# Two more feed-forward pairs by seven half-size products, a reordered hand-over, and norm sums inside a loop

## The reference, cut to what matters

```
h = rmsnorm(x, norm_ffn_pre)
u = dwconv3(h @ w_up, conv_w)            # w_up: 1024 x 5632; width-3 convolution over the tokens
gate, val = split(u, 2)                  # 2816 = 22 x 128 columns each
x = x + rmsnorm((silu(gate) * val) @ w_down, norm_ffn_post)
h2 = rms_norm(x, l0_norm); proj = h2 @ w_in_2      # the second block's first projection
```

## Time and profile before

| what | us |
|---|---|
| median of 3 runs | 1787.15 |
| lowest, highest | 1786.33, 1787.56 |
| the profiled execution's own time | 1786.32 |
| its span, first to last instruction | 1784.4 |
| PE busy in the span | 1751.6 |

### The profile page before, as it was taken

How to read it: one execution, slowest core, us unless ns; L and a number is a source line. 1 busy time by engine, 2 the same in 40 slices (tenths; PEclk the granted TensorE clock), 3 DMA queues, 4 the chain that set the end, 5 groups by cost and what they waited for, 6 DMA issues and landing times.

```text
span 1784.4 us, 21029 instructions
## 1 busy us (share of the span) xinstructions
PE 1751.6 (98%) x8288; PEld 1436.9 (81%) x8288; DVE 1195.2 (67%) x1275; ACT 771.2 (43%) x984; POOL 523.4 (29%) x217
## 2 busy tenths in 40 slices
PE   8999999999999999999999999999999999999997
PEld 5778888887888888888788888787788888888786
DVE  7454677848697978878764674764576767676533
ACT  5332222255333555555432433422256666666522
POOL 3457554454121000000264345054421111211051
PEclk9999999999999999999999999999999999999999
DMA  5223222154311122222364355312301111102232
GB/s 185 112 96 118 78 77 83 37 163 151 123 71 72 59 83 94 72 83 94 130 218 148 118 190 176 130 54 77 107 30 36 36 48 36 47 12 71 89 130 94
DMA packets 59434, 170.79 MB, mean 96 GB/s; under 512 B 7632, under 2 KB 8016, under 8 KB 59344
## 3 DMA queue, kind: packets, MB, share of 16 engines
q1 hardware_dynamic: 41488, 120.67, 20.5%
q10 hardware_dynamic: 17856, 48.87, 7.4%
HBM read 131.24 MB, written 38.27 MB: 95 GB/s over the span
## 4 chain that ended last, share of the span: by engine, by line
PE 88%; DVE 6%; ACT 4%; issue 1%; DMA 1%; POOL 0%; ACTq 0%; DVEq 0%
PE psum L671 22%; PE psum L975 15%; PE psum L988 13%; PE psum L710 7%; PE psum L1099 5%; PE psum L1120 5%; PE psum L1156 5%; PE psum L1051 4%; PE psum L870 3%; PE psum L1109 3%; PE psum L692 1%; PE psum L1076 1%; DVE ptl L2341 1%; ACT pth L1714 1%; PE psum L816 1%
## 5 line engine op out<-in xcount | busy, mean ns | idle before, releaser
L583 POOL TENSOR_TENSOR wl<-wstage,wh 128x1024 fp32r<-128x1024 f32 x101 | 262.1, 2597 | 245.8 <-ACT wh L1246 205.5
L578 POOL TENSOR_TENSOR wh<-wstage,ones 128x1024 fp32r<-128x1024 f32 x52 | 126.0, 2423 | 549.0 <-PE psum L1099 307.4
L671 PE MATMUL psum<-hh,wh 128*128 128x512 f32 x608 | 194.1, 400 | 0.9 <-ACT root L1249 0.9
L671 PE MATMUL psum<-hl,wh 128*128 128x512 f32 x608 | 187.6, 390 | 0.0
L671 PE MATMUL psum<-hh,wl 128*128 128x512 f32 x608 | 187.3, 389 | 0.0
L583 POOL TENSOR_TENSOR wx<-wstage,wx 128x1024 fp32r<-128x1024 f32 x25 | 61.6, 2465 | 378.2 <-ACT wx L1246 378.2
L2099 DVE SCALAR_TENSOR_TENSOR cc<-uu,col,cc 128x1023 f32<-128x1023 f32 x88 | 128.8, 1463 | 49.0 <-ACT cc L1462 47.4
L671 PEld LDWEIGHTS psum<-hh,wh 128*128 128x128 f32 x608 | 112.2, 188 | 29.4 <-issue 6.0
L671 PEld LDWEIGHTS psum<-hl,wh 128*128 128x128 f32 x608 | 114.1, 188 | 24.2
L671 PEld LDWEIGHTS psum<-hh,wl 128*128 128x128 f32 x608 | 114.1, 188 | 24.2
L2341 DVE TENSOR_TENSOR ptl<-psum,pth 128x1024 fp32r<-128x1024 f32 x64 | 78.3, 1224 | 55.4 <-ACT pth L1714 55.4
(11 more groups left out here) (362 smaller groups left out, 4365.0 us busy)
## 6 DMA issues: line engine op xcount, KB each, us to landing
wstage<-w_units SPq DMA_DIRECT2D x161, 512.0 KB, 3.8
acts<-cc ACTq DMA_DIRECT2D x22, 512.0 KB, 2.6
hhf<-acts SPq DMA_DIRECT2D x27, 256.0 KB, 4.2
mix<-spill ACTq DMA_DIRECT2D x12, 512.0 KB, 2.6
resid<-yo SPq DMA_DIRECT2D x24, 256.0 KB, 2.0
hlf<-acts SPq DMA_DIRECT2D x17, 256.0 KB, 4.0
kq<-mix SPq DMA_DIRECT2D x16, 256.0 KB, 4.1
gates<-gspill ACTq DMA_DIRECT2D x8, 512.0 KB, 2.6
```

The lines of the kernel that those rows point to most:

```text
L578: pool.tensor_tensor(high, stage(u), ones[:, :].unsqueeze(1).to_broadcast([P, 8, P]), ALU.mult).then_inc(w_high, 1)
L583: pool.tensor_tensor(low, stage(u), high.bitcast(F32), ALU.subtract).then_inc(w_split, 1)
L671: mm = pe.matmul(out[:, t], w[:, wslot, b, :], x[part][:, xk, t], start=start and n == 0, stop=stop and n == 2)
```

## The change

`SP` goes from 7 to 5, so 17 of 22 pairs are made by seven products. The order of the switch is changed on ScalarE and VectorE: T4, and with it the evacuation and centre tap of the last old gate unit, come behind the operands of P6, P5 and P7. The jobs of `LATER` are put into four steps. T1 and T3 are rounded one pair earlier. In `next_layer` the ones-matmuls stand between k steps, and those of the second half come for both n behind k = 5. At the end of the last pair C12 is taken before the taps.

```diff
-SP = 7
+SP = 5
-SW_MADE = ("T1", "T3", "B11", "B21", "T4", "T2", "B22")
+SW_MADE = ("T1", "T3", "B11", "B21", "T2", "T4", "B22")
         def ring(u):
-            return (u + 1) % RING
+            return (u - U_L0 + 1) % RING
...
             if U_DOWN <= u < U_DOWN + DEEP:
-                return product_done(FT - 1, ("P5", "P5", "P2", "P5", "P4")[u - U_DOWN])
+                return product_done(FT - 1, ("P5", "P5", "P5", "P4", "P2")[u - U_DOWN])
...
             def next_layer(n, base, places, emptied, after, sum_bank, y_sum):
                 pe.wait_ge(*emptied(sum_bank))
-                norm_sum_half(n, 0, sum_bank)
+                if n == 2:
+                    norm_sum_half(n, 0, sum_bank)
                 for j in range(4):
...
                     for k in range(KT):
+                        if n == 1 and j == 0:
+                            pe.wait_ge(h_lo, KT + k + 1)
                         mm = half_products(bank(2 * j), places[j], k, 0, k == 0, k == KT - 1)
+                        if n == 1 and (j, k) == (0, 1):
+                            norm_sum_half(n, 0, sum_bank)
                         if (j, k) == after:
                             pe.wait_ge(*emptied(7))
                             sum_half(1, 7, *y_sum)
...
-                pe.wait_ge(half_tile, n)
-                norm_sum_half(n, 1, 0)
+                    if k == 5:
+                        pe.wait_ge(half_tile, n)
+                        norm_sum_half(n, 1, 0)
                 pe.wait_ge(half_root, 2 * n)
...
-                       lambda bk: (evac, E_OUT + KT + TILE_BANK.index(bk) + 1), (0, 1), 3,
+                       lambda bk: (evac, E_OUT + KT + TILE_BANK.index(bk) + 1), (0, 3), 3,
```

ScalarE's stream:

```diff
+                if p == 2:
+                    right_high("T1", KT + 1, (unit_done, U_FF + 5))
                 if p == 3:
-                    right_high("T1", KT + 1, (unit_done, U_FF + 5))
-                if p == 4:
                     right_high("T3", KT + 2)
...
             right_high("B11", KT, (halves_done, 1))
             right_high("B21", KT)
-            right_high("T4", KT + 4, (sw_lo, made("B11", 1)))
-            old_centre(SP - 1, 0)
             product_high(SP, "P6")
             product_high(SP, "P5")
             right_high("T2", KT + 3, (unit_done, U_SW))
             product_high(SP, "P7")
+            right_high("T4", KT + 4, (sw_lo, made("B11", 1)))
+            old_centre(SP - 1, 0)
             product_high(SP, "P4")
             snap(SP, 0)
             old_centre(SP - 1, 1)
```

VectorE's stream:

```diff
-            LATER = (((0, 1), (2, 3)), ((4, 5), (6, 7)), ("T1", "T3"), ("T2", "T1 low"), ("T4", "T3 low"))
+            LATER = (((0, 1, 2, 3), (4, 5, 6, 7)), ("T1", "T3"), ("T2", "T1 low"), ("T4", "T3 low"))
...
             right_low("B11", 0, 1)
             right_low("B21", 0, 1)
-            right_low("T4", 0, 1)
-            projected(SP - 1, 0)
             product_low(SP, "P6")
             product_low(SP, "P5")
             right_low("T2", 0, 1)
             product_low(SP, "P7")
+            right_low("T4", 0, 1)
+            projected(SP - 1, 0)
             product_low(SP, "P4")
             projected(SP - 1, 1)
...
             taken_part(FT - 1, "C22")
             a_low(0)
+            taken_part(FT - 1, "C12")
             taps(FT - 1, 1, 0)
             a_low(1)
-            taken_part(FT - 1, "C12")
             taps(FT - 1, 0, 1)
```

## The result

The changed kernel takes **1791.26 us**, the median of 11 runs (1790.4 to 1792.6); the kernel before took 1786.85 us on the same chip (11 runs, 1786.05 to 1787.57). The ratio is 1.0025 with an interval of 1.0017 to 1.0033: slower by 4.4 us, with 24 matmuls fewer. The prediction was 1791.8. The profiled execution took 1791.1, its span is 1789.3.

The account below looks back on a forecast made before the run. PE, busy 98% of the span, was taken as the bound, at 0.227 us a matmul. -5.4 - 1.1 + 9.7 + 1.6 = +4.8 on 1786.32 gave 1791.1, with 0.8 for the median 1791.8 us; range 1784.5 to 1795.5.

Parts of the forecast that it names:

- The matmuls, -5.4: Two more pairs by seven products: 12 matmuls fewer each, 24 x 0.227 us, so -5.4 us.
- The norm sums, -1.1: In `next_layer` at n = 1, PE's stall on the last square and its restart go: -1.1 us; n = 2 worth 0.
- VectorE, E = 540.5: Before the switch, VectorE's jobs spread over four old pairs, the fourth `gated_unit` ending at 540.5.
- The switch, +9.7: First product to 61st matmul: 23.9 us instead of 14.15, of it 7.8 idle before P6, 0.8 before P1, the rest clock.
- T: The time PE reaches its first product at the switch, predicted 544.6.
- the floor of ScalarE's chain: At the switch, ScalarE's work alone lets the copy for P6 end no sooner than T + 9.8.
- The clock's price: Behind the wait before P6, a slow stretch loses 1.6 us; without it the sum would be 0.9 less.
- The tail, +1.6: End of the last pair: C12's wait goes, but taps beside GpSimd's splits delay step k = 1 to 884.7, +1.6 us.
- VectorE is early: Rival at the switch: E before 536.5, ScalarE's floor holds, 1784.5 to 1786.8 us; chance 0.18.
- the tail's bad case: End of the last pair: a split falls between the taps, +1.6 us; otherwise -0.7.
- The copy not late: Rival at the switch: the stall before P6 is under 1 us, 1779.4 us; chance 0.10.
- Worse: Rival: slow stretches after the switch and after the wait at step k = 1, or E two us later: 1793.5 to 1796; chance 0.12.

Follow-up runs that it names:

- run 10: Run 9's kernel with SP = 7 again, so 15 pairs by seven products and 24 matmuls more: 1787.08 us, ratio 1.0003.
- run 9: Run 8's kernel with the gains of the first 512 tokens applied while VectorE is idle before the last norm's root: 1780.69 us, ratio 0.9972.
- run 2: The changed kernel with the first bank copy, for P6, ahead of T4 and the centre tap on ScalarE: 1792.11 us, ratio 1.0029.
- run 3: The changed kernel with P4's high part and the first copy ahead of T4, the second behind T4, both before the centre taps: 1791.68 us, ratio 1.0026.
- run 7: The changed kernel with the eight gains on only 64 of 1024 tokens, the others left out: 1787.45 us, ratio 1.0001.
- run 11: The changed kernel with the early gains of run 9 and no other edit, nothing left out: 1787.16 us, ratio 1.0002.
- run 5: The changed kernel with the old order at the switch on ScalarE and VectorE, but SP = 5: 1790.31 us, ratio 1.0022.
- run 6: The changed kernel with 30 matmuls into an unused bank in front of P6, keeping PE at work: 1791.88 us, ratio 1.0023.
- run 4: The changed kernel with C12 behind `a_low(1)` at the end of the last pair, as before: 1789.22 us, ratio 1.0013.
- run 8: The changed kernel with copies and next pair's operands ahead of the old unit's work, and C12, `a_low(1)`, taps at the end: 1785.87 us, ratio 0.9989.
- run 1: The kernel before with only the norm-sum edits in `next_layer`: 1785.3 us, ratio 0.9994.

## Why the prediction was right

**The matmuls, -5.4.** 24 fewer in the page; the products from 572 to 868 run some 1306 matmuls in 296.00 us, 0.227 each, with VectorE busy 237 of them (a window's count takes in those that lap over its edges, here 1308; so do the 337 and 1166 of the earlier trace rows, which the prediction divides to 0.226). Run 10 against run 9 is the clean test: -6.4 measured in the median.

**The norm sums, -1.1.** The wait is gone, and the sum on the last square's row comes at 436.99 without idle. The second half's sum stands at 469.18; less the 1.1 us of the later start it is 468.1, the predicted 468.1. The reciprocal at 471.82 is 470.7 in the prediction's count, as predicted. For n = 2 the edit is worth nothing, as put down: the stretch in which it lies is 0.1 longer.

**VectorE, E = 540.5.** `gated_unit` ends at 541.2; with the later start 540.1 in the prediction's count. In between, again less the 1.1 us, the first gain starts at 475.85 (475.85 predicted), and the jobs of pairs 0 to 2 end at 497.1, 510.0 and 527.1 (497.4, 510.4, 527.4). The gains beside splits and without are 10.22 + 4.87 = 15.1 us, against 9.6 + 5.7 put down, and the two splits of pair 2 fall on its taps as written.

**The switch, +9.7: measured +9.5.** T was 545.74 (544.6 and the 1.1 of the start), the copy ended at 559.2 (T + 13.5, predicted T + 14.1), P6 started at 559.32, after 7.34 us of wait (7.8). The first product came 0.56 us after T, with 0.40 of idle for B11 (0.8). The clock behind the wait was at 0.50 for nine matmuls 0.43 apart, 1.8 us (1.6 put down). The 61st matmul had no wait of its own, since PE came later than VectorE's low part; the prediction had them 0.7 us apart the other way and then let P7's end set it, which is what happened. T + 23.7 against T + 23.9. Runs 2 and 3 show that the copy is the first of three things late, runs 7 and 11 that the lateness is VectorE's down to the floor of ScalarE's chain.

One thing in the prediction's account of the switch does not hold. It has the change's new order add the long chain (T4 behind T2, T2 behind the last old unit). Run 5 has the old order and waits 6.7 us. The size came out right because the prediction also took VectorE as late, and with VectorE this late such a wait stands in either order, 7.3 us in the new one and 6.7 in the old. The new order's own part is the floor, the 4.4 us that are left in runs 7 and 11 with VectorE early. That the old order would leave less is likely, since the copy of the kernel before is done 4.2 us behind T (592.84 and 0.58 long, T = 589.26), but it is not shown: no run has the old order, `SP = 5` and an early VectorE together.

**The clock's price.** Behind the wait 1.8 us are lost by the rows, but run 6, which has no slow stretch there, gets only 1.0 us earlier to P1, as VectorE comes next. The prediction had that too: 0.9 less without a slow stretch. By the Trainium skill ("TensorE: Matmul & The Clock Gate", Part 1: The HAM clock gate) the slow stretch behind a long idle is certain, since it has the throttled state as the default; the profiles of the runs with 4.4, 6.0, 6.5, 6.7 and 7.3 us of idle all have it. After the 2.25 us at 888.41 there is none, 24 matmuls in 5.72 us, but behind the same wait runs 3 and 6 have one.

**The tail, +1.6: measured +1.2.** C12 frees the bank in time and both taps meet a split, as put down; 6.29 us against 6.5. Step k = 1 starts at 883.28 before, where the prediction's working had 883.1. Run 4 undoes the edit and gets 2.0 us back in the median, 1.2 of it by its waits. The Trainium skill ("SBUF — State Buffer", Who interferes with whom) has GpSimd share a port pair with VectorE under a lock; two taps of 6.29 us beside splits of 2.41 and 2.91, against 2.60 without a split, agree with the sharing, and so do taps of 4.62 and 4.61 beside splits of 3.44 and 3.50. Who held the ports when, no row shows.

**What was luck.** The terms as measured are -5.4, -1.1, +9.5 and +1.2, with the -0.2 between them +4.0, against the +4.8 that was put down. The rest of the profiles' 4.8 belongs to the executions and not to the change: the later start (+1.1), the absent slow stretch at 1291 (-1.6), the slower end of the span (+1.0), and some 0.3 in small pieces. That profiles and prediction agree to a tenth is luck; the difference of the medians, 4.4, lies between the 4.0 and the 4.8. Also, +4.8 on 1786.32 and the 0.8 make 1791.9 and not 1791.8.

**The rivals.** "VectorE is early" was made true in runs 7 and 11: 1787.45 and 1787.16, where the prediction's bounds for it were 1784.5 to 1786.8. They are 0.7 and 0.4 us outside the upper one, which is for the tail's bad case, the one these runs have. "The copy not late" was priced at 1779.4; run 9 comes near it with 1780.69. It took more than moving the copy: the prediction priced that rival as if one place were late, and three were. "Worse" was two slow stretches, one after the switch and one after the wait at step k = 1: the profile of run 3 has just these two.

## What to carry to other kernels

A reordering that serves one consumer must be read to the end of the queue. Ask for each instruction that it passes, and for those behind, when the next reader needs it. Here PE stood 7.3 us for a 0.6 us copy behind a tap, and moving the copy alone uncovered two more waits of 6.5 and 6.0. When a wait moves without shrinking, the late engine is further up. Look for idle time on it before the last dependency, and fill that with the part of its work that does not depend on it: eight operations more there and the orders of run 8 turned a ratio of 1.0025 into 0.9972. Cutting PE's work also cuts the cover of the engines that run beside it, so count the jobs that must fit before the hand-over along with the matmuls saved.

## What the runs showed of the hardware

The stretches at the lower clock differ from execution to execution with the same instructions. At the start of the span the granted clock rises, and the distance of the matmuls halves, near 11.5 us before and near 13.7 us after; at the same matmul the difference is 1.1 us (31.94 and 33.05). Over all thirteen profiles the rise lies between 11.5 and 14.5 us.

Every wait of PE of 4.4 to 7.3 us, in seven profiles, was followed by a slow stretch, with six to ten distances of 0.43 us between matmuls. Short ones were followed by one in some executions only. Behind the wait of 2.2 to 2.3 us at step k = 1 of `down`, the profiles of runs 3 and 6 have eight slow matmuls, those of the changed kernel and of runs 2, 5, 7 and 11 none. Behind the wait of 1.8 us near 1290, the profiles of the kernel before and of runs 6, 7 and 10 have eight, run 5 has them behind the next wait of 1.8 us, and the other eight none. The changed kernel, at the start and behind its wait of 1.8 us (for which the window 1290 to 1296 above has PEclk 1.00):

```profile
33.05 0.64 PE L702 MATMUL psum<-xin,rkw 128*32 128x512 f32 x4
...
1295.26 0.47 PE L1105 MATMUL psum<-knh,qnh 128*128 128x512 f32 x1 [1.82 <-DVE knl L2347]
```

Each such stretch costs 1.2 to 2.0 us, so two of them are about the spread of a kernel's runs (1.8 us in run 10's eleven, 3.2 in run 8's). That they make the spread is a reading: only one execution of each kernel has a profile. The Trainium skill ("TensorE: Matmul & The Clock Gate", Part 1) says that the number of slow matmuls at a kernel's start varies from run to run with the gate's phase; the thirteen starts here agree.

It also limits what could be shown. Run 6 removed about 1 us at the switch, and in its profiled execution two later slow stretches took 3.2 us. Whether removing one stretch makes a later one more likely stays open: run 10, whose switch has no long wait either, has one at 1291, and runs 1, 8 and 9 have none.
